# A diffusion-transformer block pair on one core: a new order of the work around the third tile of the second FFN pass

## What is computed

```python
def _conv_ffn(h, w_in, conv_w, conv_b, w_out, grid):
    u, g = jnp.split(h @ w_in, 2, axis=-1)
    g = _dwconv_grid(g, conv_w, conv_b, grid)
    return (jax.nn.silu(g) * u) @ w_out
```

## Time and profile before

| | us |
|---|---|
| median of 3 runs (lowest, highest) | 2458.89 (2456.41, 2461.95) |
| the profiled execution | 2454.94 |
| its span, first to last instruction | 2453.0 |
| one loop tile of the second pass on PE (products and `down`) | 30.03 |
| from the end of `down(0)` to the start of `down(1)` | 37.43 |

### The profile page before, as it was taken

How to read it: one execution, slowest core, us unless ns; L and a number is a source line. 1 busy time by engine, 2 the same in 40 slices (tenths; PEclk the granted TensorE clock), 3 DMA queues, 4 the chain that set the end, 5 groups by cost and what they waited for, 6 DMA issues and landing times.

```text
span 2453.0 us, 35946 instructions
## 1 busy us (share of the span) xinstructions
PE 2349.1 (96%) x13630; PEld 1921.7 (78%) x13630; DVE 1671.3 (68%) x2156; ACT 815.2 (33%) x1187; POOL 894.6 (36%) x448
## 2 busy tenths in 40 slices
PE   7989999999999999999999998889979999999996
PEld 5557777787778778999889997767658888888884
DVE  4477888888888875553454306723757777889986
ACT  3642111111112125563443333333623333333333
POOL 0012122221212125663322005630576666666653
PEclk9999999999999999999999999989989999999998
DMA  8651212221122244653121238811211111111113
GB/s 345 232 198 78 86 44 84 86 86 64 65 86 86 82 175 160 219 180 113 55 75 59 71 108 218 230 52 69 69 44 57 55 51 51 51 60 69 68 43 137
DMA packets 106689, 255.10 MB, mean 104 GB/s; under 512 B 8928, under 2 KB 62816, under 8 KB 92128
## 3 DMA queue, kind: packets, MB, share of 16 engines
q1 hardware_dynamic: 89024, 228.56, 27.0%
q10 hardware_dynamic: 17568, 25.17, 2.8%
HBM read 223.68 MB, written 30.02 MB: 103 GB/s over the span
## 4 chain that ended last, share of the span: by engine, by line
PE 86%; DVE 5%; ACT 3%; DMA 2%; POOL 2%; issue 2%; SPq 0%; ACTq 0%; DVEq 0%; POOLq 0%
PE ps L737 18%; PE ps L739 17%; PE ps L738 17%; PE ps L1371 5%; PE ps L1373 5%; PE ps L1372 5%; PE ps L1123 2%; PE ps L1124 2%; PE ps L1125 2%; PE ps L839 1%; PE ps L1276 1%; PE ps L774 1%; PE ps L872 1%; PE ps L1014 1%; PE ps L790 1%
## 5 line engine op out<-in xcount | busy, mean ns | idle before, releaser
L3014 POOL TENSOR_TENSOR w_lo<-raw,w_hi 128x2048 fp32r<-128x2048 f32 x57 | 266.8, 4681 | 651.7 <-ACT w_hi L1645 291.3
L737 PE MATMUL ps<-hx_hi,w_hi 128*128 128x512 f32 x848 | 338.2, 399 | 2.5 <-ACT mix_out_c L1799 1.0
L739 PE MATMUL ps<-hx_lo,w_hi 128*128 128x512 f32 x848 | 331.3, 391 | 0.0
L738 PE MATMUL ps<-hx_hi,w_lo 128*128 128x512 f32 x848 | 331.2, 391 | 0.0
L2421 DVE TENSOR_TENSOR y_x<-y_x,ps 128x1024 f32<-128x1024 f32 x176 | 214.7, 1221 | 61.4 <-PE ps L739 56.6
L2403 DVE SCALAR_TENSOR_TENSOR acc<-ps,fcv,acc 128x945 f32<-128x945 f32 (+2 forms) x176 | 215.0, 1222 | 37.1 <-ACT acc L1689 16.0
L2926 DVE TENSOR_TENSOR y_x<-y_x,ps 128x512 f32<-128x512 f32 x304 | 206.9, 687 | 40.8 <-PE ps L739 40.8
L2873 DVE SCALAR_TENSOR_TENSOR acc<-ps,fcv,acc 128x945 f32<-128x945 f32 (+2 forms) x176 | 215.0, 1222 | 16.2 <-DVE acc L2873 2.3
L737 PEld LDWEIGHTS ps<-hx_hi,w_hi 128*128 128x128 f32 x848 | 159.8, 188 | 40.1 <-DVE hx_lo L2560 2.5
L739 PEld LDWEIGHTS ps<-hx_lo,w_hi 128*128 128x128 f32 x848 | 159.8, 188 | 34.0
L738 PEld LDWEIGHTS ps<-hx_hi,w_lo 128*128 128x128 f32 x848 | 160.0, 189 | 30.5
(11 more groups left out here) (414 smaller groups left out, 5616.9 us busy)
## 6 DMA issues: line engine op xcount, KB each, us to landing
raw<-in_ffn_w SPq DMA_DIRECT2D x44, 1024.0 KB, 6.6
modw<-in_modw SPq DMA_DIRECT2D x48, 512.0 KB, 7.0
raw<-in_ffn_w SPq DMA_DIRECT2D x44, 512.0 KB, 5.7
f_raw<-in_ffn_w SPq DMA_DIRECT2D x22, 1024.0 KB, 5.1
modw<-in_modw SPq DMA_DIRECT2D x21, 1024.0 KB, 4.8
raw<-in_mlstm_w SPq DMA_DIRECT2D x14, 1024.0 KB, 5.3
fw_raw<-in_ffn_w SPq DMA_DIRECT2D x22, 512.0 KB, 3.7
vch<-v_scr SPq DMA_DIRECT2D x18, 512.0 KB, 4.4
```

Source lines behind the costliest of these rows:

```text
L737: pe.matmul(out, whi, hhi, start=first, stop=False)
L738: pe.matmul(out, wlo, hhi, start=False, stop=False)
L739: return pe.matmul(out, whi, hlo, start=False, stop=last)
L3014: pool.tensor_tensor(w_lo[:, slot, 0:2048], raw[:, slot, 0:2048], w_hi[:, slot, 0:2048].bitcast(F32), ALU.subtract)\
```

## The change

- ACT, tile 2: u2's high part is made late in `tile(2)` and no longer ahead of the token sums' high parts. `out_high(1)` comes right behind `keep_a`; s4's high part behind the copy of s1; silu(1), `gated_high(1)` and `finish(2)` come ahead of all of tile 3's high parts.
- POOL, tile 2 and `parts(3)`: u2's low part is made last, s3's sum ahead of s4's low part, s3's low part between the halves of t3_lo; then `gated_low(1)` and `out_low(1)` come ahead of tile 3's parts (`fourth=True`).
- PE: the products s1, s2 and s3 of tile 2 wait for the low parts of their token sums in two halves (`low`), not for the whole.
- SP: `out_in(1)` comes ahead of the loop, and each `out_in` stands one place sooner against the `halves_in` in the queue; `mod_half` stands between them in tiles 14 to 18.
- `MADE_THIRD` is the order in which tile 2's low parts are counted.

```diff
-MADE_THIRD = ("s1", "g1", "g2", "u2", "s2", "s4", "s3")
+MADE_THIRD = ("s1", "g1", "g2", "s2", "s4", "s3", "u2")
...
             mod_half(0)
+            out_in(1)
             with sp.Fori(0, 6) as i:
                 for e in range(2):
                     halves_in(i * 2 + (3 + e))
-                    out_in(i * 2 + (1 + e))
+                    out_in(i * 2 + (2 + e))
             for j in range(13, FT - 1):
                 if j + 2 < FT:
                     halves_in(j + 2)
-                out_in(j)
-                if 14 <= j <= 18:
-                    mod_half(j - 13)
+                    if 14 <= j <= 18:
+                        mod_half(j - 13)
+                    out_in(j + 1)
...
-            def product(name, made, third=False):
+            def product(name, made, third=False, low=None):
...
                 for k in range(KH):
+                    if low is not None and k % 2 == 0:
+                        pe.wait_ge(sem("pool_low"), low + k // 2 + 1)
...
-                if third:
-                    pe.wait_ge(sem("pool_low"), SECOND["pool_low"] + 12)
-                product("s1", made("s1"), third)
+                product("s1", made("s1"), third, SECOND["pool_low"] + 10 if third else None)
...
-            for name in ("g1", "g2", "u2"):
+            for name in ("g1", "g2"):
                 part_high(name, 2, True)
...
+                if not (third or last):
+                    part_high("g1", j + 1)
+                out_high(j - 1)
+                done("s1")
+                act.activation(fprod[:, par, TH:TX], ps[:, BANK_B, :], ACT.Copy).then_inc(sem("act_moved"), 1)
                 if third:
                     part_high("s4", j, True)
-                elif not last:
-                    part_high("g1", j + 1)
-                if not third:
-                    out_high(j - 1)
-                done("s1")
-                act.activation(fprod[:, par, TH:TX], ps[:, BANK_B, :], ACT.Copy).then_inc(sem("act_moved"), 1)
...
                 if third:
                     part_high("s3", j, True)
-                    part_high("g1", j + 1)
-                    out_high(j - 1)
+                    part_high("u2", j, True)
+                    silu(j - 1)
+                    gated_high(j - 1, 1 - par)
+                    finish(j, par, gate_first)
+                    for name in ("g1", "s1", "s2", "s4", "s3", "g2", "u2"):
+                        part_high(name, j + 1)
+                    return
...
-            def parts(j, par):
-
+            def parts(j, par, fourth=False):
+
+                if fourth:
+                    gated_low(j - 2, par)
+                    out_low(j - 2)
                 part_low("g1", j)
-                out_low(j - 2)
+                if not fourth:
+                    out_low(j - 2)
```

More of the change, by code:

```diff
@@ L1442, in products @@
                 pe.wait_ge(sem("dve_moved"), j * 3 + (summed - 2))
-                if third:
-                    pe.wait_ge(sem("pool_low"), SECOND["pool_low"] + 12)
-                product("s1", made("s1"), third)
+                product("s1", made("s1"), third, SECOND["pool_low"] + 10 if third else None)
                 pe.wait_ge(sem("act_moved"), j * 4 + (moved + 1))
-                if third:
-                    pe.wait_ge(sem("pool_low"), SECOND["pool_low"] + 14)
-                product("s2", made("s2"), third)
+                product("s2", made("s2"), third, SECOND["pool_low"] + 12 if third else None)
                 pe.wait_ge(sem("act_moved"), j * 4 + (moved + 2))
@@ L1452, in products @@
                 pe.wait_ge(sem("act_moved"), j * 4 + (moved + 3))
-                if third:
-                    pe.wait_ge(sem("pool_low"), SECOND["pool_low"] + 16)
-                product("s3", made("s3"), third)
+                product("s3", made("s3"), third, SECOND["pool_low"] + 14 if third else None)
                 if not (third or last):
@@ L3146, in parts @@
                 part_sum("s4", j)
-                gated_low(j - 2, par)
+                if not fourth:
+                    gated_low(j - 2, par)
                 part_low("s2", j)
@@ L3186, in _ @@
                 moved(x_lo["t4"][:, k:k + 2, :], x21_at[:, k:k + 2], x_hi["t4"][:, k:k + 2, :].bitcast(F32))
-            part_low("u2", 2, True)
             for k in (0, 2):
@@ L3193, in _ @@
                 moved(x_lo["t2"][:, k:k + 2, :], x_val["t2"][:, k:k + 2, :], x_hi["t2"][:, k:k + 2, :].bitcast(F32))
+            part_sum("s3", 2, True)
             part_low("s4", 2, True)
-            part_sum("s3", 2, True)
-            part_low("s3", 2, True)
             for k in (0, 2):
@@ L3199, in _ @@
                 moved(x_lo["t3"][:, k:k + 2, :], x_val["t3"][:, k:k + 2, :], x_hi["t3"][:, k:k + 2, :].bitcast(F32))
-            parts(3, 1)
+                if k == 0:
+                    part_low("s3", 2, True)
+            part_low("u2", 2, True)
+            parts(3, 1, True)
             with pool.Fori(0, FT // 2 - 2) as i:
```

## The result

The changed kernel took 2478.42 us (median of 7 runs, 2471.81 to 2485.91) where the kernel before took 2458.32 (7 runs beside them, 2456.41 to 2461.95). The ratio is 1.0089, with an interval of 1.0072 to 1.0106: slower by 20 us, and outside the range of 2449 to 2470. Its runs are also further apart, 14 us where those of before are within 5.5.

What follows compares the result with a forecast made beforehand. The prediction took the loop to be bound by TensorE, busy all 30.03 us of a tile. It summed -8.5 (third tile) + 12.75 (loop) = +4.2, forecast +3.5: 2462 us against the 2458.89 median, range 2449 to 2470.

Steps and rivals of the forecast that it cites:

- The third tile: Tile 2's stretch between down(0) and down(1): silu(1) no longer waits for tile 3's weights; down(1) starts 15.3 us sooner.
- 1.1 us were added for the two engines' meeting: Before gated_low(1): allowance on GpSimd for VectorE's gate product, 1.26 us beside idle GpSimd and 2.22 beside busy, plus hand-over.
- The tile behind it: Tile 3: its late low parts delay tile 4's weights and stall s4, leaving 8.5 us of the 15.3 gained.
- s4's stall: In tile 3, s4 starts at 1835.6 instead of 1831.25, a new TensorE stall of 4.35 us.
- the 2.4 us for a fall of the clock: Tile 3: behind s4's gap the clock falls to 1.2 GHz, so twelve slower matmuls add 2.4 us.
- The loop: Tiles 4 to 20: f_raw queues behind fw_raw and comes 3.06 us late for ScalarE; 12.75 us lost.
- I take 0.75 a tile: TensorE's stall per loop tile over 17 tiles, ends 0.5 and 1.05; 12.75 us lost, 8.5 to 17.9.
- f_raw lands at T + 6.56: Loop: both loads issued at T + 0.36, T being the tile's start on TensorE; the burst takes 6.2 us.
- the load behind takes longer: Rival in the loop: f_raw lands half a microsecond later, stall 1.25 a tile, +12.8 us or 2471.7; chance 0.13.
- At no cost: Five loop tiles: modh comes in the same burst, but behind f_raw, adding nothing to the loss.
- The ways: From late f_raw to TensorE: s1's copy for s4, stall 0.5; silu, gate product and gated_low for down, stall 0.75.
- The sum: Whole kernel: -8.5 + 12.75 = +4.2 us, forecast as +3.5, with term bounds of -2 to +11.

Runs made afterwards that it cites:

- the kernel with the old order: Changed kernel with the loop's input weights' load again ahead of the output weights' load; only tile 1's output weights still go ahead: 7.3 us faster than the kernel before.
- three steps: On the old-queue-order kernel with GpSimd gaps, successive reorderings for tile 3 alone: ScalarE's copies ahead, silu ahead, then gated_high and gated_low(2) ahead; the last 2448.07 us.
- the kernel with f_raw first: Against the kernel with the old order: halves' load ahead of output weights', but held until the same down product is through; 2464.61 us, ratio 1.0022.
- (c): Old-queue-order kernel with GpSimd gaps and ScalarE's copies and silu ahead in tile 3, plus gated_high and gated_low(2) ahead of tile 4's token sums; 2448.07 us.
- the old order from tile 14 on: Changed kernel with SyncE's old queue order from tile 14's output weights on, new order before; tiles 15 to 19 back at 30.03 us.

## Why the prediction was wrong

- **The third tile: right, slightly large.** 15.3 us were forecast at the start of `down(1)`. It came 11.05 sooner, 13.9 with the 2.87 by which the profile of after was late beforehand. What is missing is the gate product: 1.1 us were added for the two engines' meeting, and VectorE was held 4.4 us (5.66 - 1.26). It is the first row to check in this profile, and 2.22 was no bound: there VectorE met one operation of GpSimd, here three.
- **The tile behind it: right in kind, too dark.** 8.5 us were to be left; 10.8 were. s4's stall was 2.57 instead of 4.35, and the 2.4 us for a fall of the clock did not come. That term is real (the kernel with the old order shows it behind 3.40 us), but that it stayed away here is not explained by the shorter stall: a stall of 2.54 us brought it in another kernel and one of 3.13 did not. This part of the 10.8 is luck.
- **The loop: the step that failed.** "I take 0.75 a tile", 12.75 us in all, "0.5 and 1.05 are the ends". That is 12.0 for tiles 4 to 19, and they lost 29.1 us. Of the 17.1 too many, 6.8 are the landing's and 10.3 the modulation's.
  - *The landing.* "f_raw lands at T + 6.56" was made from the one burst in the trace. It is near the middle of the seventeen (6.32 to 9.23 behind the tile's start, the middle one 6.64), and the price was near too: tiles 4 to 11 lost 0.96 each. But tiles 12 and 13 lost 6.5 together. The rival "the load behind takes longer", at 0.13, had the right direction, though it spread half a microsecond over all tiles. The rate was right, 410 GB/s; the tail at 27 GB/s was not in the sum at all, and 0.75 was the middle of bounds that knew no tail.
  - *The tiles of modulation.* "At no cost" was said of modh's load, and that is so (f_raw was used 6.1 to 6.5 us behind the first issue in tiles 15 to 19, as elsewhere); nothing was said of VectorE's four `macc_x`, two of which found, before, GpSimd's pause ahead of `gated_low` (2.33 us). With f_raw late they missed this pause, and each tile lost 2.5 us: 14.79, more than the whole of the loop's term. This is the larger part of the miss, and no rival of the prediction named it.
- **The ways.** Two were given; a third through `up_second` and u2's bank was as short. Cutting the first gained nothing.
- **The sum.** -10.81 + 14.31 + 14.79 + 0.74 is +19.0 beside the forecast +3.5, and the measured difference of the medians is 20.1.

What stays open: why one DMA engine falls behind in some bursts and not in others. The view of DMA issues gives the landing of every f_raw, waited for or not. In the fourteen traces, tiles 3 to 21, it landed 4.7 to 5.7 us behind its own issue in 183 of the 184 loads that were issued with no other of SyncE's loads under way (6.5 in the one left), and 5.0 to 8.1 us, with 5.7 as the middle, in the 82 that stood behind another. So the tail is nearly always that of a load behind another one, and not quite bound to it. It was not tried whether a third place in the queue, or a split of the 1 MB, shortens it.

## What to carry to other kernels

A load that is asked for behind another one in the same queue had a tail here, not a landing time: take its slack from the latest of many such bursts, and if the trace has only one, let that one be the lower bound. When a load becomes late by more than its slack, look at every engine behind it and at every kind of tile, those with extra work on VectorE above all, before giving a price per tile. And a wait that is moved in one tile must be followed to the last engine that needs the same late input: here it took three steps, of which the first two gained nothing and the third some 3 us in the trace.

## What the chip showed that was not expected

- A VectorE operation with two inputs in SBUF (128x1024) took 1.26 us beside an idle GpSimd, 2.26 with pauses between GpSimd's operations, and 5.66 and 5.64 beside three of them back to back; a 128x256 one took 2.51 beside a GpSimd operation of 2.40. The Trainium skill (GPSIMD Engine Reference, Specifications) names contention for VectorE operations "with two SBUF inputs". The trace agrees. It also shows who paid: in the third tile GpSimd's operations kept their 1.28 and 2.40 us and VectorE got through when a pause came; with pauses one of GpSimd's 2.40 became 3.17; and in tile 16 VectorE's product got in between two operations without a pause (1.98 us), and GpSimd's sum took 2.31 instead of 1.30.
- 1 MB behind 512 KB in one queue was there 6.0 to 8.9 us behind the first issue, and in front of it 5.0 to 5.7 behind its own, in both cases at some 410 GB/s while it ran.
- The length of a gap does not say by itself whether TensorE's clock falls, nor when. Behind gaps of 2.54, 3.40, 3.99, 4.08 and 5.12 us the first matmul took 0.77 to 0.79 us, as at 1.2 GHz. Behind 4.14 us (tile 3 of the kernel with f_raw first) it took 0.50, and the slow ones came 0.7 us later. Behind 3.01 us (tile 12 of the changed kernel) and 2.00 us (tile 4 of (c)) the first ones took 0.39 to 0.49, at 2.4 GHz, and 1.4 and 1.9 us later came eight at the slow pace, 1.6 us in all. Behind 2.57 us (tile 3 of the changed kernel) and 3.13 us (tile 3 with the old order from tile 14 on) none was slow. The prediction, which tied the fall to gaps of 4 us, could not have priced this.
